# Spreading the bf16 copies of the attention gate's weights over two attention stages of a hybrid decoder layer

## What is computed

```python
a = rms_norm(h, norm1_g)
q, k, v, u, sv, gates = split(a @ w_in)           # 9216 columns
o = diff_attention(rope(norm(q)), rope(norm(k)), v, lam)   # 8 heads, causal
att_branch = (rms_norm(o) * 0.8) @ w_att_out
sgu_branch = spatial_gating(gelu(u), gelu(sv)) @ w_sgu_out
g_att, g_sgu = split(sigmoid(gates + b_gate))     # 2048 columns each
h = h + (g_att * att_branch + g_sgu * sgu_branch) @ w_out
```

## Time and profile before

| | |
|---|---|
| time, three runs | 3678.46, 3699.12, 4313.88 us; median 3699.12 |
| the profiled execution | 3677.86 us |
| its span on the slowest core (core 3) | 3676.1 us; the eight cores 3668.9 to 3676.1 |
| PE busy | 3603.9 us, 98% |
| VectorE, ScalarE, GpSimd busy | 38%, 29%, 7% |
| granted TensorE clock, mean | 0.996 to 0.997 on all cores |
| DMA: weight queue (Pool) | 348.15 MB, 55.1% of 16 engines |
| DMA: SP queue | 104.28 MB, 9.7% |

### The profile page before, as it was taken

One profiled execution on the slowest core, in us unless ns is written; L12 is line 12 of the kernel. 1 busy time (PEld: TensorE's weight loads), 2 busy tenths in 40 slices (PEclk: granted clock), 3 DMA queues, 4 the chain that ended last, 5 costly groups with the idle time before them and its releaser, 6 DMA issues.

```text
span 3676.1 us, 49881 instructions; the slowest of 8 cores (3668.9 to 3676.1 us)
## 1 busy us (share of the span) xinstructions
PE 3603.9 (98%) x18824; PEld 1720.8 (47%) x18824; DVE 1395.7 (38%) x2082; ACT 1047.9 (29%) x1688; POOL 242.1 (7%) x405
## 2 busy tenths in 40 slices
PE   7979999999999999999999999999999999999999
PEld 3434445544554455544444444444444444444444
DVE  4335334434344513324444444201135555553001
ACT  3522245324652457413222222100032222221000
POOL 0101101100001000000000000000000000000000
PEclk9989999999999999999999999999999999999999
DMA  9996997598438864497444444667975444445665
GB/s 192 153 133 165 178 153 119 141 189 147 86 85 204 146 112 92 104 218 184 75 85 71 74 84 72 144 120 131 188 191 105 73 72 80 79 71 96 120 121 109
DMA packets 82555, 455.85 MB, mean 124 GB/s; under 512 B 9232, under 2 KB 9488, under 8 KB 38544
## 3 DMA queue, kind: packets, MB, share of 16 engines
q0 software_dynamic: 47616, 348.15, 55.1%
q1 hardware_dynamic: 34560, 104.28, 9.7%
q10 hardware_dynamic: 144, 0.22, 0.0%
HBM read 727.35 MB, written 50.33 MB: 212 GB/s over the span
## 4 chain that ended last, share of the span: by engine, by line
PE 94%; DMA 3%; DVE 1%; issue 1%; ACT 0%; another core or an unknown queue 0%; POOL 0%; DVEq 0%; SPq 0%; ACTq 0%; POOLq 0%
PE ps L357 88%; PE ps L891 5%; DMA sb_wr<-w_c 1%; PE ps L412 1%; DMA sb_wr<-w_b 1%; DVE sb_scr L363 1%; DMA sb_wr<-w_t 0%; ACT sb_scr L360 0%; DMA sb_big<-x 0%; DVE sb_scr L372 0%; DVE sb_big L363 0%; PE ps L691 0%; DVE sb_rr L737 0%; DVE sb_big L372 0%
## 5 line engine op out<-in xcount | busy, mean ns | idle before, releaser
L357 PE MATMUL ps<-sb_big,sb_wr 128*128 128x512 bf16 x9216 | 2054.2, 380 | 27.4 <-DMA sb_wr<-w_c 21.9
L357 PEld LDWEIGHTS ps<-sb_big,sb_wr 128*128 128x128 bf16 x9216 | 894.1, 98 | 1070.3 <-issue 42.6
L357 PE MATMUL ps<-sb_wr,sb_big 128*128 128x512 bf16 x4864 | 1057.7, 380 | 2.3 <-DMA sb_wr<-w_t 2.3
L357 PEld LDWEIGHTS ps<-sb_wr,sb_big 128*128 128x128 bf16 x4864 | 475.4, 98 | 571.8 <-issue 5.6
L372 DVE SCALAR_TENSOR_TENSOR sb_scr<-ps,sb_pp,sb_scr 128x1023 f32<-128x1023 f32 x352 | 451.3, 1282 | 564.4 <-ACT sb_scr L360 545.1
L360 ACT ACTIVATE sb_scr<-ps,sb_pp 128x1024 f32<-128x1024 f32 x176 | 212.0, 1205 | 918.6 <-PE ps L357 918.6
L360 ACT ACTIVATE sb_scr<-ps 128x512 bf16<-128x512 f32 (+3 forms) x768 | 375.8, 546 | 284.0 <-PE ps L357 271.5
L363 DVE TENSOR_TENSOR sb_scr<-ps,sb_scr 128x512 f32<-128x512 f32 x64 | 44.2, 692 | 553.6 <-PE ps L357 552.1
L891 PE MATMUL ps<-sb_big,sb_wr 128*128 128x512 bf16 x1024 | 224.3, 379 | 0.0
L360 ACT ACTIVATE sb_scr<-sb_big 128x512 bf16<-128x512 f32 (+2 forms) x101 | 69.7, 690 | 453.2 <-DVE sb_big L372 447.6
L357 PE MATMUL ps<-sb_scr,sb_big 128*128 128x512 bf16 (+3 forms) x640 | 179.3, 347 | 9.2 <-ACT sb_scr L360 8.7
(11 more groups left out here) (93 smaller groups left out, 1217.1 us busy)
## 6 DMA issues: line engine op xcount, KB each, us to landing
sb_wr<-w_up POOLq DMA_DIRECT2D x88, 1024.0 KB, 9.8
sb_wr<-w_c POOLq DMA_DIRECT2D x82, 1024.0 KB, 10.7
sb_wr<-w_t POOLq DMA_DIRECT2D x48, 1024.0 KB, 14.0
sb_wr<-w_dn POOLq DMA_DIRECT2D x40, 1024.0 KB, 12.7
sb_wr<-w_b POOLq DMA_DIRECT2D x32, 1024.0 KB, 10.0
sb_wr<-c_s POOLq DMA_DIRECT2D x30, 1024.0 KB, 8.3
sb_big<-x SPq DMA_DIRECT2D x32, 512.0 KB, 30.0
h_s<-sb_big SPq DMA_DIRECT2D x32, 512.0 KB, 15.4
```

What stands on the lines that cost most here:

```text
L357: S.add("pe", lambda e: e.matmul(out, lhsT=lhsT, rhs=rhs, start=start, stop=stop, **kw), reads=reads, writes=[PS(bank)])
```

## The change

Where the copies are issued, and as a consequence which slabs the first merge can read as copies. In tile 0 the copies of ga0, ga1, ga2, ga3 go out behind gs0, gs2, gs4, gs6. In tile 1 those of ga4 to ga7 go out behind gs0, gs2, gs4, gs6. The merge of tile 0 reads ga4 to ga7 as f32. The number of copies stays eight.

```diff
             for b in range(8):
-                k = b if ti == 0 else b + 6
-                if ti < 2 and k < (6 if ti == 0 else 8):
+                if ti < 2 and b % 2 == 0:
+                    k = 4 * ti + b // 2
                     extra[len(plan)] = [(k, wc_d[12 + k, 0])]
                 wplan(f"gs{b}", wc_d[20 + b, 0], 16, 256)
             for b in range(4):
                 wplan(f"sgu{b}", wb_d[4 + b, 0], 8, 512)
             for g in range(4):
                 for b in (2 * g, 2 * g + 1):
-                    if ti == 0 and b >= 6:
+                    if ti == 0 and b >= 4:
                         wplan(f"ga{b}", wc_d[12 + b, 0], 16, 256)
                     else:
                         wcached(f"ga{b}", b, 16, 256)
```

## The result

| | before | after |
|---|---|---|
| time, median of 11 runs each | 3678.46 us | 3660.43 us |
| profiled span, slowest core | 3676.1 (core 3) | 3659.4 (core 0) |
| spans of the eight cores | 3668.9 to 3676.1 | 3649.6 to 3659.4 |
| PE busy | 3603.9 | 3597.2 |
| mean granted clock | 0.996 to 0.997 | 0.999 |

The ratio is 0.995, with a 95% interval of 0.9935 to 0.9964: 13 to 24 us faster, well outside the noise and well inside 2%. So of the 18.0 us between the table's two medians some 16.5 are the change's.

What follows compares the result with a forecast made beforehand. PE is busy nearly everywhere but waits 21.9 us for weights queued with six copies in the first attention. Sum: -22.8 + 1.5 + 6.1 + 0 = -15.2, from 3677.9 to 3662.7 us; 8-in-10 range 3652 to 3692.

Steps and rivals of the forecast that it cites:

- The queue's arithmetic: First attention: transfers land in issue order, 6.2 us for a slab, 16.2 us for a copy and slab.
- PE's wants: First attention: when PE is ready for each slab; waits of 2.0 us before gs5 and 4.3 before gs7.
- the rate: Matmuls after a wait run at the lower clock, losing 0.45 us for each us waited.
- Engines that lose their cover: First attention: ScalarE and VectorE lose the time in which they caught up; 1.5 us charged, between 0 and 5.
- Rival (a): First attention and merge: ScalarE and VectorE hold PE (5 us), the merge costs 11; 3671 us, chance 0.14.
- The merge: First merge: ga4 and ga5 as f32 give 4.2 us of waits and 1.9 of slow clock, 6.1 lost.
- the two differences of 3.3 us: First merge: extra landing time of ga4 and ga5 as f32 slabs instead of cached bf16, 3.3 us each.
- The check by the page: First merge: 6.15 us for a 1 MB load would make the f32 reads cost nothing more; 3656.6 us.
- rival (b): First merge: the f32 reads cost nothing; 3656.6 us, chance 0.14.
- The second attention: Four copies in place of two hide behind the attention's own matmuls; charged 0, bounds 0 to 3 us.
- (c): First merge: the backlog becomes short waits at slab after slab; slower, 3681 to 3693 us, chance 0.05.
- (d): First attention: the 16 us beat is a limit other than the copies, nothing changes; 3677 us, chance 0.05.

Runs made afterwards that it cites:

- tile1_no_copies: Changed kernel without the second attention's four copies, ga4 to ga7 of tiles 1 to 3 read from the copies of ga0 to ga3; 3660.5 and 3661.9 us.
- merge_reads_bf16: Changed kernel, but ga4 and ga5 of tile 0 read as bf16 from the copies of ga0 and ga1; 0.9943, 3656.4 against 3676.7 us.
- merge_f32_alone: Kernel before, with only ga4 and ga5 of tile 0 read as f32, the six copies left in place; ratio 1.003 (0.9989 to 1.0071).
- four_in_a_row: Changed kernel with the first attention's four copies behind gs0, gs1, gs2 and gs3; 0.9971 to the kernel before, 3666.0 against 3676.7 us.
- late_copies_six: Changed kernel with tile 0 copies behind gs0, gs2, gs4, sgu1, sgu3, ga0 and two in tile 1; 3655.6, 3656.8, 3662.0 us, later 0.9940.

## Why the prediction was right

Predicted 3662.7 us, measured 3660.4; a gain of 15.2 forecast and 18.0 found between the table's medians, of which some 16.5 are the change's.

**The queue's arithmetic held.** Landings in the first attention, forecast from one price for a slab and one for a pair, and read in the trace after (issue time plus time to landing of each; this core begins the stage 0.6 us later than the one of the forecast):

| | gs1 | gs2 | gs3 | gs4 | gs5 | gs6 | gs7 |
|---|---|---|---|---|---|---|---|
| forecast | 184.5 | 190.7 | 206.9 | 213.1 | 229.3 | 235.5 | 251.7 |
| measured | 185.4 | 192.0 | 207.5 | 213.8 | 229.5 | 235.9 | 252.1 |

**PE's wants** were right to about 1 us: gs5 was wanted 2.0 us before it came and was waited for 0.71; gs7 4.3 and 5.27. Together 6.0 for 6.3. The slow clock behind them was not shared out by the rate: nothing behind the 0.71 us, 5.69 x 0.5 = 2.8 behind the 5.27, where the rate would have given 2.4. That the sum is the forecast's 2.8 is luck in part.

**Engines that lose their cover:** charged 1.5. The four other kinds of wait add up to 7.9 us in the stage, 1.0 more than the 6.9 that the same view of before adds up to; it is in the wait for ScalarE's `sb_big` (2.1 for 1.0). Rival (a) asked for 5.

**The first attention's end:** the merge starts at 302.88 where it started at 324.14, read in the trace before:

```profile
324.14 6.21 PE L891 MATMUL ps<-sb_big,sb_wr 128*128 128x512 bf16 x28
```

21.3 us earlier, the forecast's number. The two are different cores, and a core by itself gains less or more: core 0 18.9 (321.77 to 302.88), core 3 24.2 (324.14 to 299.91). Over the eight cores the mean start goes from 321.6 to 300.6, 21.0 earlier, so the number stands, and that the slowest core before and the slowest after show it to the tenth is luck.

**The merge was sized too high.** The forecast set out from the profiled execution before (3677.9); like with like, the profiled execution after took 3661.1, 1.6 us under the 3662.7, and the merge accounts for that. From the start of its first ga slab to that of att3 it took 77.3 us before (324.14 to 401.44) and takes 81.8 now (302.88 to 384.69): 4.5 more, where 6.1 was charged. The waits were right on the slowest core (4.3 us for 4.2) and wrongly placed in part: att2 and ga6 waited too, so the two differences of 3.3 us came earlier in the queue than I let them. The 1.9 us of slow clock did not come on this core; its merge ran at 1.00. The rate of 0.45 us a us waited was read behind waits of 2.4 to 7.1 us in a stage in which PE also idles in between, and I carried it to waits of 0.8 to 2.1 us in a stage without any other idle. It can come there (1.7 us behind the 2.13 us wait of tile1_no_copies, and on core 2 of this very profile behind 2.27 us), but it did not come behind a 2.07 us one. Put right, the sum is -21.3 + 4.5 = -16.8; the profiled spans differ by 16.7. And over the cores the merge's waits average 1.9 us, and in the kernel before six of the eight have none: att3 without slack was a matter of the core that I read.

**The check by the page.** The rival price from the page "DMA: Bandwidth & Descriptors" of the Trainium skill, section "Bandwidth", 6.15 us for 1 MB (measured there with the pair's other core idle), would have made the merge's step free (3656.6), as rival (b) had it. The median lies between it and mine, but not for that reason: merge_reads_bf16 is 4 us faster than the changed kernel and merge_f32_alone brings waits of its own, so the two reads do differ in price, and (b) falls. By the second figure there, 358 GB/s for each core of a pair, they differ too; the prediction's estimate from it, 5.9 us for an f32 slab, is near the 6.2 between landings.

**The second attention** cost nothing, as charged: no wait in it in the profile after, none saved by taking its copies away, and the limit found by doubling them lay where the arithmetic put it. gs3 landed at 541.5 + 28.5 = 570.0 and was wanted at 577.2, with 7 us to spare where 4.7 were forecast.

**The other rivals.** (c), a chain of short waits behind the merge, did not appear: the trace has no wait for a weight behind the merge on any of the eight cores. (d) is gone with the change itself, and four_in_a_row shows the cause: two copies fewer, in the same rhythm of one copy behind each slab, brought 11 us in spite of the merge.

## What to carry to other kernels

Where transfers are served in order, price the queue and not the transfer: one landing interval with the extra transfer and one without give every later landing by addition, and set against what the consumer wants they say which waits stay, before anything is run. A copy made for later reuse belongs where the consumer's pace is slower than the queue's (here 11.8 us a slab against 6.2), spread so that each has recovered before the next; a mean DMA share of 0.8 does not say that there is room for more. And read every core before calling a slack nil, since the end goes by the worst of them and the typical loss by their mean.

## What the runs showed of the hardware that was not expected

Two things. The clock behind a short wait is not a fixed price, and not a rate either. The profiles of the kernels with an f32 slab or a late copy in the first merge have ten waits of 2.0 to 2.7 us there on cores with a mean granted clock of 0.996 and more, all in a stage that PE otherwise nearly fills. Behind five of them (2.03, 2.06, 2.13, 2.27 and 2.52 us) the matmuls lost 1.5 to 1.7 us, and behind the other five (2.05, 2.07, 2.08, 2.09 and 2.65 us) nothing. In the first attention of the kernel before, core 6 lost 1.7 us behind a wait of 1.90 us, and core 1 nothing behind one of 3.56. So two waits of the same length can differ by all of the price, and a forecast can give it a chance but no size by length.

And on one chip the clock fell in fully busy stretches, with no idle before. In late_copies_six, while PE works through the slabs of a tile without a gap:

```profile
1600.00:1640.00 40.00, 40.00 (x177) 17.67 (x176) 9.69 (x14) 10.12 (x28) 1.58 (x3) 0.95 1.02 254
...
1602.00:1604.00 2.00, 2.00 (x10) 0.87 (x9) 0.96 (x2) 0.72 (x2) 0.00 (x0) 0.94 1.15 295
1604.00:1606.00 2.00, 2.00 (x9) 0.87 (x8) 0.53 (x2) 0.72 (x2) 0.00 (x0) 0.81 1.17 199
1606.00:1608.00 2.00, 2.00 (x10) 0.78 (x8) 0.59 (x2) 0.72 (x2) 0.00 (x0) 0.81 0.86 156
1608.00:1610.00 2.00, 2.00 (x11) 0.90 (x10) 0.49 (x1) 0.72 (x2) 0.00 (x0) 0.98 0.92 231
```

PE is busy for all of the 40 us, at a mean granted clock of 0.95, which is 2 us lost. Most of the stretch is at 1.00, and two short pieces of it, here and at 1634 to 1638, read a flat 0.81. That is neither of the two levels given ahead, and whether it is a level of its own or an even mixture of the two, these rows do not say. Core 1 shows 0.81 at the same times, cores 4 to 7 stay at 1.00. The changed kernel shows a fall at 1600 us on the same chip as well (0.96 over 20 us); in its first profile, on another chip, there is none. Over the whole run of late_copies_six cores 0 and 1 have a mean clock of 0.998 where cores 4 to 7 have 1.000, which is some 7 us by estimate, as much as the steps studied here. What causes it, these runs do not show.
